# Sparse attention on one Trainium2 core: the scores of compressed keys in four matmuls a head, the two products added by VectorE

## What is computed

```python
def nsa_mixer(u, table, w_in, pe_k, w1_k, w2_k, pe_v, w1_v, w2_v, w_out):
    ...
    k_cmp = compress(kc, pe_k, w1_k, w2_k)        # [b, 31, G, 64]
    v_cmp = compress(vc, pe_v, w1_v, w2_v)
    ...
        dist_c = t[:, None] - cmp_end[None, :]
        m_c = dist_c >= 0
        bias_c = jnp.transpose(table_g[rel_bucket(dist_c)], (2, 3, 0, 1))
        s_c = jnp.einsum('bqgjd,bcgd->bgjqc', qblk, k_cmp).astype(jnp.float32) + bias_c
        p_c = jax.nn.softmax(jnp.where(m_c, s_c, NEG), axis=-1) * jnp.any(m_c, axis=-1)[:, None]
        o_c = jnp.einsum('bgjqc,bcgd->bqgjd', p_c.astype(v_cmp.dtype), v_cmp)
    ...
    o = gate[..., 0:1] * o_c + gate[..., 1:2] * o_s + gate[..., 2:3] * o_w
    return (o * silu(z)) @ w_out
```

## Time and profile before

| | us |
|---|---|
| median of 3 runs | 2083.43 (2083.24 to 2084.54) |
| the profiled execution | 2085.87 |
| its span, first to last instruction | 2084.6 |
| TensorE busy | 2044.4 (98%) |
| VectorE busy | 964.6 (46%) |
| ScalarE busy | 780.6 (37%) |
| GpSimd busy | 324.9 (16%) |
| TensorE's mean granted clock | 0.995 of full speed |

### The profile page before, as it was taken

How to read it: one execution, slowest core, us unless ns; L and a number is a source line. 1 busy time by engine, 2 the same in 40 slices (tenths; PEclk the granted TensorE clock), 3 DMA queues, 4 the chain that set the end, 5 groups by cost and what they waited for, 6 DMA issues and landing times.

```text
span 2084.6 us, 26714 instructions
## 1 busy us (share of the span) xinstructions
PE 2044.4 (98%) x10149; PEld 1658.4 (80%) x10149; DVE 964.6 (46%) x1968; ACT 780.6 (37%) x1552; POOL 324.9 (16%) x497
## 2 busy tenths in 40 slices
PE   7999999999999999999999999999998999999998
PEld 5887888888888886788888888888787888777766
DVE  4438434443354344435534443364435664535455
ACT  4226332222232223333322222243336884435453
POOL 2103100000002120000110000041003764312211
PEclk9999999999999999999999999999998999999999
DMA  5330243333324331132243333225321103323212
GB/s 178 102 98 14 61 134 91 95 98 94 99 79 137 99 97 46 51 101 93 68 135 100 95 97 100 93 84 160 117 78 55 32 22 102 114 74 109 67 46 81
DMA packets 96766, 187.32 MB, mean 90 GB/s; under 512 B 8407, under 2 KB 16639, under 8 KB 96512
## 3 DMA queue, kind: packets, MB, share of 16 engines
q1 hardware_dynamic: 90288, 164.35, 26.1%
q0 software_dynamic: 6352, 21.27, 3.2%
HBM read 181.33 MB, written 4.26 MB: 89 GB/s over the span
## 4 chain that ended last, share of the span: by engine, by line
PE 91%; ACT 5%; DVE 2%; issue 1%; POOL 1%; DMA 0%; SPq 0%; ACTq 0%; DVEq 0%; POOLq 0%
PE bank L750 62%; PE bank L786 10%; PE bank L1261 5%; PE bank L1020 2%; PE bank L1182 1%; PE bank L1159 1%; PE bank L824 1%; PE bank L1275 1%; ACT sc L1804 1%; PE bank L849 1%; PE bank L1005 1%; PE bank L1091 1%; PE bank L1298 1%; ACT xn L1798 1%; PE bank L1148 1%
## 5 line engine op out<-in xcount | busy, mean ns | idle before, releaser
L1975 DVE TENSOR_TENSOR wl<-raw,wh 128x1024 fp32r<-128x1024 f32 x306 | 375.8, 1232 | 774.3 <-ACT wh L1378 773.4
L1378 ACT ACTIVATE wh<-raw 128x1024 fp32r<-128x1024 f32 x306 | 321.0, 1053 | 827.3 <-PE bank L750 785.3
L750 PE MATMUL bank<-hTh,wh 128*128 128x512 f32 (+2 forms) x1200 | 467.5, 390 | 0.2 <-issue 0.2
L750 PE MATMUL bank<-hTl,wh 128*128 128x512 f32 (+2 forms) x1200 | 466.9, 389 | 0.0
L750 PE MATMUL bank<-hTh,wl 128*128 128x512 f32 (+2 forms) x1200 | 466.9, 389 | 0.0
L750 PEld LDWEIGHTS bank<-hTh,wh 128*128 128x128 f32 (+2 forms) x1200 | 223.9, 187 | 48.5 <-issue 0.3
L750 PEld LDWEIGHTS bank<-hTh,wl 128*128 128x128 f32 (+2 forms) x1200 | 223.9, 187 | 48.4
L750 PEld LDWEIGHTS bank<-hTl,wh 128*128 128x128 f32 (+2 forms) x1200 | 223.9, 187 | 47.9
L750 PE MATMUL bank<-wh,hTh 128*128 128x512 f32 x400 | 156.5, 391 | 0.1
L750 PE MATMUL bank<-wh,hTl 128*128 128x512 f32 x400 | 155.7, 389 | 0.0
L750 PE MATMUL bank<-wl,hTh 128*128 128x512 f32 x400 | 155.6, 389 | 0.0
(11 more groups left out here) (383 smaller groups left out, 3111.9 us busy)
## 6 DMA issues: line engine op xcount, KB each, us to landing
raw<-in_ffn_w_in SPq DMA_DIRECT2D x88, 512.0 KB, 3.7
raw<-in_ret_w_in SPq DMA_DIRECT2D x48, 512.0 KB, 3.8
raw<-in_ffn_w_out SPq DMA_DIRECT2D x44, 512.0 KB, 3.7
raw<-in_diff_w_in SPq DMA_DIRECT2D x32, 512.0 KB, 3.8
raw<-in_fox_w_in SPq DMA_DIRECT2D x24, 512.0 KB, 4.0
raw<-in_nsa_w_in SPq DMA_DIRECT2D x20, 512.0 KB, 3.7
raw<-in_ret_w_out SPq DMA_DIRECT2D x16, 512.0 KB, 3.7
raw<-in_fox_w_out SPq DMA_DIRECT2D x8, 512.0 KB, 3.6
```

The lines of the kernel that those rows point to most:

```text
L750: i = pe.do.matmul(dst, x, y, start=first and k == 0 and q == 0, stop=stop)
L1378: act.do.activation(M.hl[n % HL_SLOTS][0][:, 0:m], M.raw[n % RAW_SLOTS][:, 0:m], ACT.Copy).then_inc(*T.up("act_hi", n))
L1975: dve.do.tensor_tensor(wl[:, 0:m], M.raw[n % RAW_SLOTS][:, 0:m], wh[:, 0:m].bitcast(F32), ALU.subtract).then_inc(*T.up("dve_lo", n))
```

## The change

The two tiles of compressed keys become one, `a.kc` [128, 4 groups, 2, 32]: for each group the 32 high columns and then the 32 low ones; `a.kcmp` and `a.kcml` are now views of it, written by the same instructions as before. For each query block TensorE issues one matmul with the 64 columns of the head's own group, which leaves the two products side by side in PSUM. VectorE copies the low one to SBUF (`a.cs`, new), waits for itself, adds the high one from PSUM, waits for itself, and the four maxima read the sum from SBUF.

```diff
@@ -311,7 +311,8 @@
-            a.kcmp, a.kcml = sb(stack, "kcmp", [128, 4, 32], F32R), sb(stack, "kcml", [128, 4, 32], F32R)
+            a.kc = sb(stack, "kc", [128, 4, 2, 32], F32R)
+            a.kcmp, a.kcml = a.kc[:, :, 0, :], a.kc[:, :, 1, :]
@@ -326,6 +327,7 @@
+            a.cs = sb(stack, "cs", [128, 4, 32])
@@ -1131,8 +1133,7 @@
         pe.wait_ge(*at("dve_kcmp", "lo"))
         for i in range(4):
             qs = slice(i * 128, i * 128 + 128)
-            pe.do.matmul(M.bank[3][:, qs], query(M, h)[:, qs], a.kcmp[:, :, :], start=True, stop=False)
-            t = pe.do.matmul(M.bank[3][:, qs], query(M, h)[:, qs], a.kcml[:, :, :], start=False, stop=True)
+            t = pe.do.matmul(M.bank[3][:, i * 128:i * 128 + 64], query(M, h)[:, qs], a.kc[:, h // 4, :, :], start=True, stop=True)
         t.then_inc(*up("pe_cmp", ("scores", h)))
         pe.free[3] = [("dve_cmp", (h, "max"))]
@@ -2552,10 +2553,15 @@
             dve.wait_ge(*at(f"bt{h % 4}", h))
             if h >= 2:
                 dve.wait_ge(*at("pe_cmp", ("turned", h - 2)))
+            both = M.bank[3][:, :].rearrange("p (i w c) -> p i w c", i=4, w=4)
+            dve.do.tensor_copy(a.cs[:, :, :], both[:, :, 1, :]).then_inc(*up("dve_cmp", (h, "low")))
+            dve.wait_ge(*at("dve_cmp", (h, "low")))
+            dve.do.tensor_tensor(a.cs[:, :, :], both[:, :, 0, :], a.cs[:, :, :], ALU.add).then_inc(*up("dve_cmp", (h, "sum")))
+            dve.wait_ge(*at("dve_cmp", (h, "sum")))
             for i in range(4):
-                k, c = cmp_blocks(i), i * 128 + h // 4 * 32
+                k = cmp_blocks(i)
                 bias = bass.AP(tensor=a.BT[h % 4][:, :].tensor, offset=96 + 128 * i, ap=[[512, 128], [-16, k]])
-                dve.do.tensor_tensor_reduce(a.sc[h % 2][:, i, 0:k], M.bank[3][:, c:c + k], bias, -1.0, BIG, ALU.add, ALU.min,
+                dve.do.tensor_tensor_reduce(a.sc[h % 2][:, i, 0:k], a.cs[:, i, 0:k], bias, -1.0, BIG, ALU.add, ALU.min,
                                             a.scs[h % 2][:, i, 0:1]).then_inc(*up("dve_cmp", (h, "max")))
```

## The result

| | before | after |
|---|---|---|
| median | 2083.92 us (4 runs, 2083.24 to 2084.54) | 2097.93 us (4 runs, 2096.54 to 2099.50) |
| ratio | | 1.0067, 95% interval 1.0055 to 1.0079 |
| the profiled execution, its span | 2085.87, 2084.6 | 2096.54, 2095.2 |
| TensorE busy, instructions | 2044.4 | 2038.0, 64 matmuls fewer |
| VectorE busy | 964.6 | 980.5 |

What follows compares the result with a forecast made beforehand. TensorE held 91% of the chain, alternating with ScalarE in sparse attention. Seven pairs x (0.12 + 0.34) = 3.2, + 0.56, - 0.84 gave +2.9 us, forecast 2086.3 us (+0.14%), range 2081.8 to 2088.8.

Steps and rivals of the forecast that it cites:

- Two kinds of head: Sparse attention: the chain runs through the compressed-score matmuls in even heads only; in odd heads it leaves TensorE before them.
- the pair: VectorE's added copy and addition before the four maxima, each followed by a wait for itself: 0.29 + 0.04 us each.
- X: Time VectorE's added copy, addition and self-waits cost per head: 0.66 us, ends 0.50 and 0.76.
- The rival of a free self-wait: VectorE's self-waits cost nothing, each new instruction 0.22 us: -0.4 us, 2083.0; chance 0.10 (same).
- even heads from 4 on: Compressed exponentials start 0.12 us later per even head, as VectorE's added work outweighs TensorE's 0.45 saved.
- odd heads, without the hold: Compressed exponentials start 0.34 us later per odd head, all on the path; the maximum starts only 0.22 early.
- up to head 2's boundary: Start of the stage: head 0 slips by 0.56 us, head 1 gives back 0.84, head 2 slips by 0.12.
- The term for head 1, -0.84: Head 1 runs at TensorE's 1.2 GHz level, matmuls 0.21 apart on the chain: four removed give back 0.84 us.
- The stall at the eight transposes: TensorE's wait before L1159 x8 grows from 0.42 to about 1.0 us in even heads, 1.2 in odd ones.
- the dearer pair: Rival: VectorE's copy or self-waits cost more, deciding above X = 0.72 to 0.75: +4.9 us, 2088.3; chance 0.22 (slower).
- Narrow matmuls: Rival: VectorE's added work is hidden and narrow matmuls cost 0.075 us each: -5.1 us, 2078.3; chance 0.07 (faster).
- the clock rival: TensorE's longer stall before the eight transposes drops its clock to 1.2 GHz: +14 us a stretch; chance 0.03 (slower).

Runs made afterwards that it cites:

- e4: The changed kernel without copy and addition, maxima reading the high product from PSUM, low part of the keys left out: 2079.52 us, ratio 0.9980.
- e1: The changed kernel, but VectorE writes the sum back to PSUM and the four maxima read it there: 2088.73 us, ratio 1.0023.
- e2: The changed kernel, but GpSimd does its block with subtraction L646 two tiles later: 2088.44 us, ratio 1.0023.
- b1: The kernel before, unchanged, profiled once more: 2083.72 us, span 2082.4.
- e5: The changed kernel, with GpSimd's subtraction L646 as two instructions of 256 columns: 2096.89 us, ratio 1.0064.
- f1: The kernel before, with ScalarE's copy of the transposed tile ahead of the compressed exponentials: 2083.43 us, ratio 0.9999.
- f3: The changed kernel, sum in SBUF, with ScalarE's copy of the transposed tile ahead of the compressed exponentials: 2089.62 us, ratio 1.0028.

## Why the prediction was wrong

**What was right.** Two kinds of head, and which of them contains TensorE's saving: e4 has -0.44 in the even head (0.43 worked out) and -0.02 in the odd one (0). The prices of the pair: copy 286 ns, addition 291, each with 0.03 to 0.04 behind it (1663.53 to 1663.85 to 1664.18 in head 8), X = 0.69 against 0.66. Its effect: with the hold absent, e1 has +0.13 in the even head (0.12) and +0.34 in the odd one (0.34), a pair of 19.18 where "steady stretches of 19.2" was written. Its total was not: e1 and e2, without the hold, came out 5.5 and 5.2 us above the kernel before, where 2.9 was forecast. Of the 5.3 us between the profiles of b1 and e1, 3.1 lie between the boundaries of heads 2 and 15, 0.3 ahead of them and 1.9 behind. The rival of a free self-wait is refuted: the copy, without a wait, starts 0.08 before the end of the maximum ahead (1663.53 against 1663.61), the addition, with one, 0.03 after the end of the copy. The Trainium skill ("VectorE: DVE Perf Modes", section "The DRAIN you can't avoid") has a semaphore after each of eight copies cost nothing extra; these shorter instructions don't bear that out.

**The step that failed** is the sentence "The four reductions now read SBUF in place of PSUM; the trace has none of that size, so I leave their price and take 0.05 off at the low end." I saw the change of memory and asked only for its speed, in the direction of a gain. I didn't ask who else reads SBUF at that time. "No GpSimd work is moved" was true, and misled: the work of another engine need not move to be in the way. The row was in the trace of before, one engine beside those I had printed in the earlier trace rows:

```profile
1671.29 0.18 DVE L2558 CUSTOM_DVE_ANT_0 sc<-bank,bt 128x23 f32<-128x23 f32 x1
1671.36 1.27 POOL L644 TENSOR_TENSOR hTl<-prodn,hTh 128x512 fp32r<-128x512 f32 x1 [0.74 <-ACT hTh L1825]
...
1671.40 0.20 DVE L2558 CUSTOM_DVE_ANT_0 sc<-bank,bt 128x31 f32<-128x31 f32 x1
```

The last maximum starts 0.04 us after L644 and, with its input in PSUM, takes its usual 0.20: nothing is held there. From L644's row the loss could have been worked out: by the prediction's own steps the tile's maximum starts at 1670.54, the first compressed maximum 0.34 + 0.66 later at 1671.54, and L644 runs until 1672.63. Ended by then in place of 0.17 after its start, that is 0.92 us in each of seven odd heads, 6.4 us on top of the forecast's 2.9, some 2093.

The Trainium skill had the rule, and I did not weigh it: "SBUF — State Buffer", section "Who interferes with whom", says that a VectorE instruction with two inputs in SBUF contends with a GpSimd instruction that reads SBUF. Of the port pair that the two engines share it says there that it is an exclusive lock, and, in its point on VectorE's two-port modes, that whoever issues first gets it for the whole instruction. All runs here agree: 1.15 us beside L646 with `cs` and `bt` in SBUF (after), 0.17 with one in PSUM (e1), 0.17 without L646 (e2), and a hold that ends with each half (e5).

**The sum, term by term.** From b1's span of 2082.4 to after's of 2095.2 are 12.8 us (the medians differ by 14.0; the other 1.2 is not in this pair of profiles):

| term | predicted | measured |
|---|---|---|
| even heads from 4 on | 6 x 0.12 = 0.7 | 6 x 0.16 = 1.0 |
| odd heads, without the hold | 7 x 0.34 = 2.4 | 7 x 0.34 = 2.4 |
| odd heads, the hold | not in it | 7 x 1.00 = 7.0 |
| up to head 2's boundary | 0.56 - 0.84 + 0.12 = -0.2 | 1605.85 - 1605.30 = +0.55 |
| behind the loop | 0 | 356.9 - 355.0 = +1.9 |

The term for head 1, -0.84, was taken from matmuls at the 1.2 GHz level. That was a state of that one execution: b1 has 1.00 granted at 1589 with the same code (and 0.50 again from 1593 to 1595), and after has 1.00 from 1591 on. Measured against the first profile of before, the same row would be 1605.85 - 1607.51 = -1.66 in place of +0.55, so a single pair of profiles doesn't settle it. A gain that hangs on a low clock in one profile should have had half its size at most. The last term is again the clock, not work. Behind the loop, in after, a wait of 1.45 us is followed by a dip (the matmul, then the stretches of after):

```profile
1965.82 0.56 PE L1299 MATMUL bank<-vd,pTd 128*128 128x128 f32 x2 [1.45 <-DVE vd L2624]
```

```profile
1964.00:1966.00 2.00, 0.55 (x3) 0.31 (x4) 2.00 (x3) 0.85 (x1) 0.00 (x0) 1.00 0.00 0
1966.00:1968.00 2.00, 2.00 (x7) 1.61 (x8) 2.00 (x9) 0.86 (x5) 0.45 (x1) 0.53 0.80 212
1968.00:1970.00 2.00, 2.00 (x7) 1.58 (x6) 1.05 (x2) 0.29 (x2) 1.14 (x3) 0.62 0.84 206
```

The last two stretches lack 2 x 0.47 + 2 x 0.38 = 1.7 us of full clock, nearly the whole term. In b1 the same place comes eleven us earlier, after the same wait of 1.45, and keeps its clock (TensorE is busy for 0.99 of the 2 us from 1954 on, then throughout):

```profile
1954.00:1956.00 2.00, 0.99 (x5) 0.90 (x6) 2.00 (x3) 0.04 (x1) 0.00 (x0) 1.00 0.27 61
1956.00:1958.00 2.00, 2.00 (x10) 1.50 (x8) 2.00 (x10) 1.15 (x5) 1.26 (x3) 1.00 0.78 238
```

The part behind the loop is 356.9 us in after and e1, and 355.0 in before, b1 and e4. The dip is also in f1 (0.59 and 0.55 from 1954 to 1958) and in f3. f1 has the code of before there, so it isn't the change of this kernel; what decides it is open.

**What the changed profile was to show.** The stall at the eight transposes was to be 1.0 us in even heads and 1.2 in odd ones; e1 has 0.79 and 1.08. The steps fit all the same, so 0.1 to 0.2 of TensorE's saving lies in another place of the head. In even heads it is a wait of 0.24 us for ScalarE's copy in the middle of the six transposes ahead of these eight (1660.34 in e1; in e4 too, where 0.21 + 0.24 makes the 0.45 saved); in odd heads I haven't found it. L1805's idle time, 0.55 and 0.34 worked out, is 0.49 in head 8 of after and 0.29 in head 9 of e1. In after's odd head it is 1.30, the 1.0 of the hold on top. **The other rivals:** the dearer pair (X above 0.72) did not occur. Narrow matmuls are not cheaper: with 64 columns four of them start 0.11 apart, as those of 128 and 256. The clock stayed at 1.00 through stalls of 2.09 us in the steady stretches of after. But in e5 it fell once to 0.50, for some 4 us right behind the same stall, and that step was 1.6 us longer: what the clock rival names does occur, if far smaller than the 14 us a stretch that I gave it.

## What to carry to other kernels

When a change moves an operand from PSUM to SBUF, count the SBUF inputs of each VectorE instruction afterwards; one with two of them must be laid beside GpSimd's timeline, not only beside those of its producers and consumers. A 0.17-us instruction can become as long as the GpSimd instruction it lands beside, and the way out is to leave one input in PSUM or move GpSimd's work, not to cut it in pieces. And a saving counts only in the heads (or stages) whose chain passes through it: here half of them, which left 4 us to win and an addition that cost more.

## What the runs showed of the hardware that I had not expected

- A VectorE instruction with two SBUF inputs was held by GpSimd's subtraction, which reads SBUF and began before it, until that was through: 1.15 us for 128x7 beside a 1.28-us subtraction, 0.60 and 0.73 beside its halves. It is recorded as a long VectorE instruction, so the wait shows up as busy time and as "issue" in the chain, never as a wait for GpSimd. GpSimd's own duration hardly changes with the hold (after against before: 1282 and 1272 ns in the mean for the first four blocks, 1282 and 1284 for the last four).
- A second VectorE instruction can get in between two GpSimd instructions that follow each other (the 0.17 at 1674.99 in e5, and so in five of seven odd heads; in the other two it was held by the second of them).
- The granted clock at a given place isn't a property of the kernel: 0.50 until 1597 in one execution of before, 1.00 from 1589 in another, which is worth 2.2 us of the span; and 1.9 us behind the loop in some executions after the same work. After a stall of 2.08 it fell once in e5, and not after the other odd heads' stalls of that length. Differences of 2 us between two single profiles of this kernel mean nothing unless the clock's rows are compared.
